# A decoder trunk on one core: the last block of features computed in two token groups of 192 and 128

## The reference

```python
x = x + 0.5 * swiglu(rmsnorm(x, g_norm[l, 2]), w_ffn_in[l, 1], w_ffn_out[l, 1])
...
y = rmsnorm(x, g_final)

def rmsnorm(x, g):
    xf = x.astype(F32)
    y = xf * lax.rsqrt(jnp.mean(xf * xf, axis=-1, keepdims=True) + EPS)
    return (y * g.astype(F32)).astype(x.dtype)

def swiglu(h, w_in, w_out):
    gu = h @ w_in
    g, u = jnp.split(gu, 2, axis=-1)
    return (jax.nn.silu(g) * u) @ w_out
```

## Time and profile before

| what | value |
|---|---|
| median of 3 runs | 1247.01 us (1245.93 to 1247.26) |
| the profiled execution, its own time | 1247.35 us |
| its span, first to last instruction | 1245.6 us |
| granted TensorE clock, mean | 0.995 of full speed |
| TensorE matmul busy | 1234.8 us, 99% of the span |
| VectorE, ScalarE, GpSimd busy | 727.1, 580.6, 80.7 us |

### The profile page before, as it was taken

How to read it: one execution, slowest core, us unless ns; L and a number is a source line. 1 busy time by engine, 2 the same in 40 slices (tenths; PEclk the granted TensorE clock), 3 DMA queues, 4 the chain that set the end, 5 groups by cost and what they waited for, 6 DMA issues and landing times.

```text
span 1245.6 us, 21960 instructions
## 1 busy us (share of the span) xinstructions
PE 1234.8 (99%) x8827; PEld 1210.0 (97%) x8827; DVE 727.1 (58%) x1125; ACT 580.6 (47%) x931; POOL 80.7 (6%) x99
## 2 busy tenths in 40 slices
PE   8999999999999999999999999999999999999997
PEld 8999999989999999999998999999997999999997
DVE  6655655575777656554564655654567485655443
ACT  5534333454556445443445554433444464544332
POOL 0000001100332000000000000000020110000010
PEclk9999999999999999999999999999999999999998
DMA  9344344533444443334544744334578734443441
GB/s 338 138 147 156 105 138 150 206 131 137 136 160 148 160 164 135 136 117 144 194 152 147 251 138 165 124 116 145 188 269 307 273 135 154 149 142 119 140 139 42
DMA packets 35465, 200.40 MB, mean 161 GB/s; under 512 B 4234, under 2 KB 4618, under 8 KB 20178
## 3 DMA queue, kind: packets, MB, share of 16 engines
q1 hardware_dynamic: 33426, 192.27, 44.3%
q0 software_dynamic: 1984, 7.38, 1.9%
HBM read 193.06 MB, written 6.57 MB: 160 GB/s over the span
## 4 chain that ended last, share of the span: by engine, by line
PE 99%; DVE 0%; DMA 0%; ACT 0%; SPq 0%; issue 0%; DVEq 0%; ACTq 0%
PE bank L514 30%; PE bank L516 29%; PE bank L515 29%; PE bank L663 1%; PE bank L664 1%; PE bank L662 1%; PE bank L994 1%; PE bank L665 1%; PE bank L666 1%; PE bank L819 0%; PE bank L954 0%; DMA x<-x_in 0%; PE bank L774 0%; PE bank L922 0%; PE bank L912 0%; PE bank L904 0%
## 5 line engine op out<-in xcount | busy, mean ns | idle before, releaser
L514 PE MATMUL bank<-h_hi,w_hi 128*128 128x320 f32 x1792 | 557.0, 311 | 2.2 <-DVE h_lo L1535 2.2
L516 PE MATMUL bank<-h_hi,w_lo 128*128 128x320 f32 x1792 | 555.4, 310 | 0.0
L515 PE MATMUL bank<-h_lo,w_hi 128*128 128x320 f32 x1792 | 555.3, 310 | 0.0
L1107 ACT ACTIVATE w_hi<-raw 128x1024 fp32r<-128x1024 f32 (+1 forms) x364 | 331.9, 958 | 443.3 <-PE bank L516 423.0
L1521 DVE TENSOR_TENSOR w_lo<-raw,w_hi 128x1024 fp32r<-128x1024 f32 (+1 forms) x364 | 388.5, 1107 | 133.6 <-ACT w_hi L1107 133.6
L514 PEld LDWEIGHTS bank<-h_hi,w_hi 128*128 128x128 f32 x1792 | 337.3, 188 | 3.7 <-issue 2.6
L515 PEld LDWEIGHTS bank<-h_lo,w_hi 128*128 128x128 f32 x1792 | 337.2, 188 | 0.1
L516 PEld LDWEIGHTS bank<-h_hi,w_lo 128*128 128x128 f32 x1792 | 337.2, 188 | 0.0
L516 PE MATMUL bank<-f_hi,w_lo 128*128 128x320 f32 x704 | 217.6, 309 | 0.0
L514 PE MATMUL bank<-f_hi,w_hi 128*128 128x320 f32 x704 | 217.6, 309 | 0.0
L515 PE MATMUL bank<-f_lo,w_hi 128*128 128x320 f32 x704 | 217.6, 309 | 0.0
(11 more groups left out here) (252 smaller groups left out, 757.9 us busy)
## 6 DMA issues: line engine op xcount, KB each, us to landing
raw<-w_in SPq DMA_DIRECT2D x86, 1024.0 KB, 4.8
raw<-w_out SPq DMA_DIRECT2D x64, 704.0 KB, 4.1
raw<-w_a SPq DMA_DIRECT2D x12, 1024.0 KB, 4.8
raw<-w_kv SPq DMA_DIRECT2D x8, 1024.0 KB, 4.8
raw<-vc_in SPq DMA_DIRECT2D x12, 512.0 KB, 7.1
raw<-kc_in SPq DMA_DIRECT2D x10, 512.0 KB, 4.4
raw<-w_oa SPq DMA_DIRECT2D x4, 1024.0 KB, 5.5
raw<-w_q SPq DMA_DIRECT2D x4, 1024.0 KB, 4.8
```

The costliest lines, as they stand in the source:

```text
L514: pe.matmul(out, wh, mh, start=first, stop=False)
L515: pe.matmul(out, wh, ml, start=False, stop=False)
L516: return pe.matmul(out, wl, mh, start=False, stop=last)
L1107: sc.activation(w_hi[:, n_at % 2, part * w:part * w + w], raw[:, raw_of(n_at) % RAW, part * w:part * w + w], ACT.Copy).then_inc(hi_done, 1)
```

## The change

The last feature block is computed in two token groups, by a new function `last_chunk`: first the 66 matmuls for tokens 0 to 191 into bank 5, then 66 matmuls, with the same stationary operands again, for tokens 192 to 319 into bank 0. The last norm is made for each group. The steps of the first group's norm are written into the matmuls of the second group: the totals ahead of its hidden block 6, the spread of the factors ahead of its hidden block 13. The steps of the second group's norm come behind the last matmul.

The loop over blocks 2 to 7 becomes a loop over 2 to 5 with block 6 written out behind it. Blocks 6 and 7 also get their gain on ScalarE (block 7 in two groups). VectorE writes the results into `raw` instead of `x`, with each group's tokens packed together, and `y_out` is stored by group: four parts of 2 blocks x 192 tokens, then two parts of 4 blocks x 128 tokens.

```diff
-        Y_PARTS = ((0, 2), (2, 4), (4, 6), (6, 7), (7, 8))
+        Y_FIRST = ((0, 2), (2, 4), (4, 6), (6, 8))
+        Y_LAST = ((0, 4), (4, 8))
@@ tensor engine
-                with pe.Fori(0, (KT - 2) // 2) as i:
+                with pe.Fori(0, (KT - 2) // 2 - (f == 3)) as i:
                     for j in (2, 3):
                         out_chunk(i * 2 + j, j, False)
+                if f == 3:
+                    out_chunk(KT - 2, KT - 2, False)
+                    last_chunk(u)
+            def last_chunk(u):
+                m = KT - 1
+                def tokens(out, g, t):
+                    s, kt = (u + FK + g // HALF) % 2, g % HALF
+                    return passes(out, w_hi[:, s, kt * 128:kt * 128 + 128], w_lo[:, s, kt * 128:kt * 128 + 128],
+                                  f_hi[:, g, t], f_lo[:, g, t], g == 0, g == FK - 1)
+                def spread(t, own, at):
+                    n = own.stop - own.start
+                    return pe.matmul(bank[7][:, at:at + n], rcol[own, t:t + 1].to_broadcast([n, 128]),
+                                     ident[own, own], start=True, stop=True)
+                pe.wait_ge(x_ready, m + (XB[3] - 1))
+                for g in range(FK):
+                    if g % HALF == 0:
+                        pe.wait_ge(lo_done, m * 2 + (u + FK + g // HALF + 1))
+                    mm = tokens(bank[5][:, 0:YA], g, slice(0, YA))
+                mm.then_inc(unit_done, 1)
+                for g in range(FK):
+                    if g == 6:
+                        pe.wait_ge(sum_done, KT * 5 + 7)
+                        pe.wait_ge(root_done, 6)
+                        for t, at in enumerate((0, YA - 128, YA)):
+                            pe.matmul(bank[6][:, 320 + t:321 + t], norm_room[:, T + at:T + at + 128], ones[:, 0:1],
+                                      start=(t == 0), stop=False, skip_group_check=True)
+                        pe.wait_ge(sq_done, KT * 6)
+                        for t, at in enumerate((0, YA - 128)):
+                            mm = pe.matmul(bank[6][:, 320 + t:321 + t], norm_room[:, 2 * T + at:2 * T + at + 128],
+                                           ones[:, 0:1], start=False, stop=True, skip_group_check=True)
+                        mm.then_inc(ssq_done, 1)
+                    if g == 13:
+                        pe.wait_ge(rcol_done, 3)
+                        spread(0, slice(0, 128), 0)
+                        spread(1, slice(256 - YA, 128), 128).then_inc(y_factor, 1)
+                    mm = tokens(bank[0][:, 0:T - YA], g, slice(YA, T))
+                mm.then_inc(unit_done, 1)
+                pe.wait_ge(sq_done, KT * 6 + 1)
+                pe.matmul(bank[6][:, 322:323], norm_room[:, 2 * T + YA:3 * T], ones[:, 0:1], start=False, stop=True,
+                          skip_group_check=True).then_inc(ssq_done, 1)
+                pe.wait_ge(rcol_done, 4)
+                spread(2, slice(0, 128), YA).then_inc(y_factor, 1)
@@ scalar engine
+            for i, own, t in ((0, slice(0, YA), slice(0, 2)), (1, slice(YA, T), slice(2, 3))):
+                sc.wait_ge(y_add, i + 1)
+                sc.activation(sq[:, 0, own], x[:, m, own], ACT.Square).then_inc(sq_done, 1)
+                sc.activation(x[:, m, own], x[:, m, own], ACT.Copy,
+                              scale=par[:, P_G + KT * N_FIN + m:P_G + KT * N_FIN + m + 1]).then_inc(y_gained, 1)
+                sc.wait_ge(ssq_done, 7 + i)
+                sc.activation(rcol[:, t], bank[6][:, 320 + t.start:320 + t.stop], ACT.Sqrt, bias=epsc[:, 0:1],
+                              scale=1.0 / D).then_inc(rcol_root, 1)
@@ vector engine
+            add_tokens(0, first, bank[5][:, 0:YA])
             ve.wait_ge(rcol_root, 1)
+            ve.reciprocal(rcol[:, 0:2], rcol[:, 0:2]).then_inc(rcol_done, 1)
             ve.wait_ge(y_factor, 1)
+            for m, e in Y_FIRST:
+                ve.wait_ge(y_gained, e)
+                if e == KT:
+                    add_tokens(1, last, bank[0][:, 0:T - YA])
+                times_factor(y_first, m, e, first)
+            ve.wait_ge(rcol_root, 2)
+            ve.reciprocal(rcol[:, 2:3], rcol[:, 2:3]).then_inc(rcol_done, 1)
+            ve.wait_ge(y_factor, 2)
+            ve.wait_ge(y_gained, KT + 1)
+            for m, e in Y_LAST:
+                times_factor(y_last, m, e, last)
```

More of the change, by code:

```diff
@@ L42 @@
 QB, SLOT, RB = 4, 32, 160
+YA = 192
 R_HALF, R_MUL, R_NEG, R_DEL, R_M0 = 0, 256, 576, 896, 904
@@ L230, in trunk_program @@
         y_factor = sem("y_factor_spread")
-        tok_first = sem("first_seven_token_totals")
+        y_add = sem("last_chunk_tokens_added")
         mo_done = sem("last_m_gathered")
@@ L343, in trunk_program @@
         XB = [0, 2 * KT, 3 * KT, 5 * KT]
-        Y_PARTS = ((0, 2), (2, 4), (4, 6), (6, 7), (7, 8))
+        Y_FIRST = ((0, 2), (2, 4), (4, 6), (6, 8))
+        Y_LAST = ((0, 4), (4, 8))
+        y_first = raw[:, 0, 0:KT * YA].rearrange("p (m t) -> p m t", t=YA)
+        y_last = raw[:, 1, 0:KT * (T - YA)].rearrange("p (m t) -> p m t", t=T - YA)
         def piece(t, q):
@@ L499, in _ @@
             ffn(3)
-            for i, (m, e) in enumerate(Y_PARTS):
+            for i, (m, e) in enumerate(Y_FIRST):
                 sp.wait_ge(y_done, i + 1)
-                sp.dma_start(y_out[:, m:e, :], x[:, m:e, :]).then_inc(s_y, 16)
-            sp.wait_ge(s_y, 16 * len(Y_PARTS))
+                sp.dma_start(y_out[:, m * YA:e * YA], raw[:, 0, m * YA:e * YA]).then_inc(s_y, 16)
+            for i, (m, e) in enumerate(Y_LAST):
+                w, at = T - YA, KT * YA
+                sp.wait_ge(y_done, len(Y_FIRST) + i + 1)
+                sp.dma_start(y_out[:, at + m * w:at + e * w], raw[:, 1, m * w:e * w]).then_inc(s_y, 16)
+            sp.wait_ge(s_y, 16 * (len(Y_FIRST) + len(Y_LAST)))
             sp.wait_ge(cn_out, 16 * H)
@@ L1070, in _ @@
             ffn(3, split_at_kt(7 * KT), None, lambda: total(5))
[L1072 to L1088, removed]
         @block.scalar
@@ L1171, in ffn @@
                     update(j_out, m - 1, norm, (x_ready, xbase + m))
-                    if f == 3 and m <= 6:
+                    if f == 3:
                         sc.activation(x[:, m - 1, :], x[:, m - 1, :], ACT.Copy,
@@ L1497, in _ @@
             sc.activation(rcol[:, 0:1], epsc[:, :], ACT.Sqrt)
-            sc.wait_ge(x_ready, 6 * KT)
             sc.wait_ge(sum_done, KT * 5 + 7)
[L1500 to L1504, removed]
+            m = KT - 1
+            for i, own, t in ((0, slice(0, YA), slice(0, 2)), (1, slice(YA, T), slice(2, 3))):
[6 more added lines that the diff above has]
+                              scale=1.0 / D).then_inc(rcol_root, 1)
         @block.vector
@@ L2067, in _, with add_tokens, times_factor @@
             ffn(3, None, 0, after_ob)
-            add_out(3, KT - 1)
+            def add_tokens(i, own, src):
+                ve.wait_ge(unit_done, U_END - 1 + i)
+                ve.scalar_tensor_tensor(out=x[:, KT - 1, own], in0=src, scalar=0.5, in1=x[:, KT - 1, own],
+                                        op0=ALU.mult, op1=ALU.add).then_inc(y_add, 1)
+            def times_factor(out, m, e, own):
+                n = own.stop - own.start
+                ve.tensor_tensor(out[:, m:e, :], x[:, m:e, own],
+                                 bank[7][:, own].unsqueeze(1).to_broadcast([128, e - m, n]), ALU.mult
+                                 ).then_inc(y_done, 1)
+            first, last = slice(0, YA), slice(YA, T)
+            add_tokens(0, first, bank[5][:, 0:YA])
             ve.wait_ge(rcol_root, 1)
-            ve.reciprocal(rcol[:, :], rcol[:, :]).then_inc(rcol_done, 1)
+            ve.reciprocal(rcol[:, 0:2], rcol[:, 0:2]).then_inc(rcol_done, 1)
             ve.wait_ge(y_factor, 1)
[L2072 to L2080, removed]
+            for m, e in Y_FIRST:
[9 more added lines that the diff above has]
+                times_factor(y_last, m, e, last)
         @block.gpsimd
@@ L2253 @@
     }
-    outs = {"y_out": (128, KT, T), "k_out": (128, H, T), "v_out": (128, 3, H, DV), "cp_out": (H, DK, DV + 1),
+    outs = {"y_out": (128, KT * T), "k_out": (128, H, T), "v_out": (128, 3, H, DV), "cp_out": (H, DK, DV + 1),
             "cs_out": (H, 128, 4, DV + 1), "m_out": (8, 1 + NB)}
@@ L2261 @@
     r = run(nc, [arrays], core_ids=[0]).results[0]
-    y = r["y_out"].transpose(2, 1, 0).reshape(T, D)
+    y = np.concatenate([r["y_out"][:, 0:KT * YA].reshape(128, KT, YA),
+                        r["y_out"][:, KT * YA:].reshape(128, KT, T - YA)], axis=2).transpose(2, 1, 0).reshape(T, D)
     k = r["k_out"].transpose(2, 1, 0)
```

## The result

| kernel | median us | ratio to before, 95% interval | span, profiled | outside the span |
|---|---|---|---|---|
| before | 1247.01 (5 runs) | | 1245.6 | 1.8 |
| changed | 1254.52 (5 runs) | 1.0062 [1.0048, 1.0077] | 1252.3 | 2.2 |

A forecast was written before the change was run, and what follows sets the result against it. TensorE, busy 99% of the span, was taken to bound the kernel. TensorE +6.33 us and tail -4.1 us gave +2.2 us on the profiled 1247.35 us: 1249.5 us, range 1246.3 to 1252.5.

The forecast's parts named there:

- What bounds it, the loads: TensorE's list counts in full; block 7's short matmuls start every 110 ns, the pace of their loads, 14.41 us together.
- the sum: Whole kernel: TensorE +6.33 us and tail -4.1 us make +2.2 us, 1249.5 us; chance as summed 0.58.
- streaming rival: Block 7: loads hide, so matmuls start every 92.6 and 65.5 ns; 1245.4 us, chance 0.15.
- handover rival: Block 7: a handover adds to each load, so matmuls start every 121.4 ns; 1251.0 us, chance 0.17.
- The records inside the second group: Second group: five totals and two spreads, 14 records at 110 ns each, add 1.54 us to TensorE.
- the covers: Second group: waits at totals and spread end 0.8 and 1.8 us early; the second weights unit has 0.85 us.
- The tail: From the last matmul's end to the span's end: 10.5 us shrinks to 6.4, -4.1 us.
- The clock: Second group: granted clock stays at 1.00, 2.4 GHz, up to the last matmul because the list is dense.
- The falling clock: Second group: half of it runs at 1.2 GHz, 33 x 110 ns more, +3.6 us, 1253.1 us; chance 0.07.

The follow-up runs named there:

- pad224: Changed kernel with the second group's matmuls streaming 224 columns instead of 128, the extra ones not read: 1249.96 us, ratio 1.0026.
- pad256: Changed kernel with the second group's matmuls streaming 256 columns instead of 128, the extra ones not read: 1250.37 us, ratio 1.0027.
- tot_wide: Changed kernel with every total of the last norm streaming 48 columns of ones instead of one: 1250.29 us, ratio 1.0022.
- tot_early: Changed kernel with the three totals of blocks 0 to 6 moved into the first group, ahead of hidden block 18: 1250.45 us, ratio 1.0029.
- pad192: Changed kernel with the second group's matmuls streaming 192 columns instead of 128, the extra ones not read: 1250.12 us, ratio 1.0026.
- norm_behind: Changed kernel with the norm of both groups behind the last matmul, no totals or spread inside the second group: 1251.42 us, ratio 1.0039.
- late8: Changed kernel with only the last 8 of block 7's 22 hidden blocks in two groups, the first 14 streaming 320 columns: 1247.83 us, ratio 1.0011.
- one_group: Changed kernel with block 7 in one group and the norm behind it, keeping ScalarE's gains, new stores and layout: 1246.19 us, ratio 0.9992.
- filler_parts: Kernel before with eight unread filler matmuls in the tail and the first result part split, six stores in all: 1246.37 us, ratio 0.9997.
- unrolled: Kernel before with blocks 6 and 7 of the last feed-forward written out behind a shorter loop: 1246.67 us, ratio 0.9997.

## Why the prediction was wrong

**What bounds it, the loads.** Right. TensorE pays for whatever is added to its list. The distance of short matmuls is that of the load, 111 ns against 110 in the sum, at 128, 192 and 224 columns alike; at 256 streaming takes over. The bounds 92.6 and 65.5 ns (streaming rival, 0.15) and 121.4 ns (handover rival, 0.17) are both excluded by the changed kernel itself, and by pad224 and pad256.

**The records inside the second group.** Nearly right. Ten records of totals took 1.09 us against 1.10. At full clock, in pad224, the way from the first to the last start is 16.52 us where 15.95 were summed. 131 distances of 111.8 ns instead of 110 make 0.24 of the difference. 0.25 lies in the first group's spreads: their four records take 0.69 us (1237.37 to 1238.06), not the 0.44 that follows from "the spread's moving side is no longer than its load". The small rest is the first matmuls behind the fp32 records. No wait in the stream was late in the changed kernel, so the covers held.

**The tail.** Right in sum: 6.5 us against 6.4. At full clock it would be 6.1 (pad224, 1241.33 to 1247.4).

**The clock.** This is the step that failed. The sum held 1.00 to the last matmul because "granted clock 1.00 wherever the list was dense, and this list is dense". A list can be dense in instructions and loads and still be thin in what streams. Nor was the sentence true of the kernel before as it stands: at its start the clock fell at 8.2 us, after TensorE had idled, and dense matmuls of 320 columns then ran at 0.50:

```profile
6.00:8.00 2.00, 0.59 (x4) 0.62 (x5) 1.29 (x3) 1.75 (x4) 0.00 (x0) 1.00 0.97 319
8.00:10.00 2.00, 2.00 (x10) 2.00 (x9) 1.88 (x4) 1.49 (x4) 0.00 (x0) 0.56 0.90 306
```

The falling clock was a rival at 0.07 and 1253.1 us, beyond the top of the range (1252.5); it was the case. It was priced at 33 matmuls, 3.6 us. In fact 34 matmuls ran at 213 instead of 111 ns, 3.5 us, the four records of the spread took 1.28 us instead of 0.69, and the last spread took 0.79 us instead of 0.49: 4.4 together. tot_wide and pad224 give back 4.2 and 4.6 us.

**The sum again.** From its first to its last matmul start block 7 took 20.47 us in the changed kernel where 15.95 were summed. 0.6 of the 4.5 us is there at full clock too (pad224), 3.9 is the clock. The last matmul and the tail took 0.3 more than summed. With 2.2 forecast and 0.5 outside the span (2.22 against 1.75 in the two profiled executions), which the prediction took as unchanged, that makes 7.5, as measured. This count starts at block 7, which begins 0.36 us earlier in the changed kernel's profiled execution; the profiled execution of the kernel before stood 0.34 us above its median, which evens this out. Without the falling clock the change still loses: tot_wide stands at 1.0022 [1.0013, 1.0032], and it, tot_early, pad192 and pad224 take 3.3 to 4.0 us more than the kernel before. The forecast of 2.5 us above the median would then have been 0.8 to 1.5 us short, with the time inside its range.

**The mechanism of the fall.** Shown: 128-column matmuls without the norm in them do not bring it about (norm_behind), the norm among 192 or 224 columns does not (pad192, pad224), nor do the ten records of totals made wider (tot_wide) or six of them moved (tot_early). It takes both in one stretch. The spreads had no part in it, since the clock fell at 1236.8 and they start at 1238.46. A trace shows one execution, but the times agree with it: every execution of the changed kernel took 1253.8 us or more, and none of the five kernels named took more than 1252.9 us. Not shown: how the chip weighs the two, and how little widening or moving would have been enough.

## What to carry to other kernels

Splitting a block of matmuls along the moving side repeats every load; where the load takes 111 ns, as for the fp32r matmuls here, a moving side of 128, 192 or 224 columns costs the same 110 to 112 ns. The slope of the earlier trace rows puts the end of this at some 236 columns, an estimate. Such short matmuls leave the array streaming little, and thin records put among them can halve the clock of a stream that never waits: look at the granted clock of the new stretch, and fill the load time with columns that need not be read, or put the thin records elsewhere. A split should cover only as many steps as the norm beside it needs (late8); here even that only came out level.

## What was not expected of the hardware

- The granted clock fell to 0.50 while TensorE was busy for all of 1232 to 1240 us, and did not come back in 9 more us, to the last matmul, of dense matmuls of 128 columns at 1.2 GHz.
- 96 more streamed columns in each of 66 matmuls made the kernel 4.6 us faster than the changed one.
- Device time less span is 1.8 us for the kernel before and 2.05 to 2.2 for every kernel with two groups. The stores and the layout (one_group, 1.81), six stores (filler_parts, 1.78) and a list longer by two blocks (unrolled, 1.78) are not the cause; the changed kernel's list is longer by three. It stays open.
